# Expert products written to PSUM instead of a held row read from PSUM, with two gather buffers that come free later

## What is computed

```
h   = x + merged @ w_o ;  hn = rms_norm(h, g_ffn)
s   = scores of 8 heads against two sets of 128 sub-keys; top 16 pairs per head -> experts e, gates g
u   = u_tab[e] ;  act = gelu(sum_d hn[d] * u[e, d])          # 128 experts for each token
v   = v_tab[e] ;  y = h + sum_e g * act * v[e, :] ;  out = rms_norm(y, g_fin)
```

## Time and profile before

| | before |
|---|---|
| median of 3 runs | 1904.86 us (1900.15 to 1910.61) |
| span of the profiled execution | 2029.6 us |
| busy: TensorE / VectorE / GpSimd / ScalarE | 1467.7 / 1202.8 / 1067.7 / 380.8 us |
| DMA over the span | mean 348 GB/s, 706 MB |
| quad 0, quad 38, quad 64, quad 96, quad 124 begin at | 388, 891, 1213, 1590, 1921 us |

### The profile page before, as it was taken

How to read it: one execution, slowest core, us unless ns; L and a number is a source line. 1 busy time by engine, 2 the same in 40 slices (tenths; PEclk the granted TensorE clock), 3 DMA queues, 4 the chain that set the end, 5 groups by cost and what they waited for, 6 DMA issues and landing times.

```text
span 2029.6 us, 18882 instructions
## 1 busy us (share of the span) xinstructions
PE 1467.7 (72%) x5470; PEld 670.5 (33%) x5470; DVE 1202.8 (59%) x3335; ACT 380.8 (19%) x923; POOL 1067.7 (53%) x1082
## 2 busy tenths in 40 slices
PE   8999998756886687768996555555555666676657
PEld 5444443443443333322442222222222233221111
DVE  1034352585577567667666776677676777687541
ACT  2113441222222222111111111211111212111101
POOL 3020000264575566766566666666666666666674
PEclk9999999976897888778997877777777777776778
DMA  9999998697999799999999989999999999998997
GB/s 329 359 310 365 362 318 304 199 323 260 389 388 362 274 375 343 396 397 375 396 364 403 376 332 344 342 365 361 368 352 368 347 352 357 354 361 332 369 369 284
DMA packets 226136, 706.43 MB, mean 348 GB/s; under 512 B 21153, under 2 KB 46657, under 8 KB 226009
## 3 DMA queue, kind: packets, MB, share of 16 engines
q0 software_dynamic: 166912, 612.40, 80.5%
q1 hardware_dynamic: 59120, 92.82, 13.2%
HBM read 700.65 MB, written 72.61 MB: 381 GB/s over the span
## 4 chain that ended last, share of the span: by engine, by line
PE 26%; DVE 23%; issue 19%; DMA 11%; POOL 9%; another core or an unknown queue 8%; ACT 1%; SPq 1%; DVEq 0%; POOLq 0%; ACTq 0%
PE bank L1059 7%; PE bank L947 4%; DVE XS L1463 4%; POOL WR L660 4%; DVE GT L1463 3%; DMA arena<-in_peer_u_dram,e_all 3%; PE bank L1175 3%; POOL XS L660 2%; DMA WR<-in_peer_v_dram,arena 2%; DVE arena L1463 2%; PE bank L1076 2%; PE bank L1196 2%; PE bank L1154 2%; DMA WR<-in_w_in_dram 2%
## 5 line engine op out<-in xcount | busy, mean ns | idle before, releaser
L1059 PE MATMUL bank<-WR,arena 128*64 128x512 f32 x1728 | 536.1, 724 | 189.8 <-issue 82.1
L660 POOL DMA_INDIRECT WR<-in_peer_v_dram,arena x432 | 427.0, 988 | 301.0 <-issue 145.4
L660 POOL DMA_INDIRECT XS<-in_peer_u_dram,e_all x258 | 269.2, 1043 | 225.7 <-DVE XS L1463 77.4
L1059 PEld LDWEIGHTS bank<-WR,arena 128*64 128x64 f32 x1728 | 146.8, 163 | 520.2 <-issue 470.2
L1463 DVE SCALAR_TENSOR_TENSOR XS<-XS,bank 128x1024 f32<-128x1024 f32 x144 | 171.2, 1218 | 41.3 <-DMA XS<-in_peer_u_dram,e_all 38.8
L1463 DVE SCALAR_TENSOR_TENSOR GT<-GT,bank 128x1024 f32<-128x1024 f32 x126 | 150.0, 1218 | 59.8 <-DMA GT<-in_peer_u_dram,e_all 45.3
L1463 DVE SCALAR_TENSOR_TENSOR XS<-XS,GT 128x1024 f32<-128x1024 f32 x114 | 137.4, 1225 | 80.1 <-DMA XS<-in_peer_u_dram,e_all 65.6
L660 POOL DMA_INDIRECT GT<-in_peer_u_dram,e_all x126 | 123.1, 977 | 52.3 <-issue 33.9
L660 POOL DMA_INDIRECT arena<-in_peer_u_dram,e_all x128 | 127.4, 995 | 42.1 <-issue 37.8
L754 ACT ACTIVATE XS<-bank 128x256 f32<-128x256 f32 (+1 forms) x90 | 36.2, 405 | 469.1 <-remote 267.7
L1076 PE MATMUL bank<-WR,XS 128*128 128x512 f32 x256 | 116.0, 607 | 0.4 <-ACT arena L754 0.4
(11 more groups left out here) (234 smaller groups left out, 2122.9 us busy)
## 6 DMA issues: line engine op xcount, KB each, us to landing
out_dram<-in_cache_a_k_dram POOLq DMA_DIRECT2D x8, 4064.0 KB, 54.6
out_dram<-in_cache_a_v_dram POOLq DMA_DIRECT2D x8, 4064.0 KB, 55.4
WR<-in_w_in_dram SPq DMA_DIRECT2D x8, 2048.0 KB, 25.7
GT<-in_w_peer_q_dram SPq DMA_DIRECT2D x14, 1024.0 KB
WR<-in_w_out_dram SPq DMA_DIRECT2D x6, 2048.0 KB
WR<-in_peer_v_dram,arena POOLq DMA_INDIRECT x432
WR<-in_w_branch_a_dram SPq DMA_DIRECT2D x6, 1024.0 KB, 7.6
WR<-in_w_branch_b_dram SPq DMA_DIRECT2D x6, 1024.0 KB, 9.7
```

The costliest lines, as they stand in the source:

```text
L660: nc.gpsimd.indirect_dma_start(dst, None, table, bass.IndirectOffsetOnAxis(ap=idx, axis=0))\
L1059: last = nc.tensor.matmul(b[c][R * j:R * j + R, :], diag[p // QUAD % 4][:, s % 4, :], V[V_AT[s]][:, c * CHUNK:(c + 1) * CHUNK], start=Fals ...
```

## The change

The held copy goes, with its semaphore. Every SCALAR_TENSOR_TENSOR reads `hidden[t]` from SBUF in all quads. From quad 38 on its unread products go to the two PSUM banks (`aside`) instead of over the u row, in the sampled quads too. As all of them write the same place, each one from the second on waits until the one before has finished (`u_used` >= s). `hidden[1]` is in use until quad 63 and `hidden[2]` until quad 95, so the buffers that lie on them come later: the u ring has 7 buffers from quad 44 (with `O` as the seventh) and 8 from quad 66; the v ring has 10 from quad 56 and 12 from quad 98. `ring` hands new buffers out first and then keeps the order of use.

```diff
-HELD_FROM = {t: max(t * TILE_Q, 38) for t in range(1, TILES)}
+ASIDE_FROM = 38
@@
-WIDER_U, WIDER_V, WIDEST_V = 44 * QUAD, 56 * QUAD, 80 * QUAD
-def u_buffer(s):
-    return s % 4 if s < WIDER_U else s % 8
-def v_buffer(s):
-    if s < WIDER_V:
-        return s % 8
-    return (s - WIDER_V) % 10 if s < WIDEST_V else (s - WIDEST_V + 10) % 12
+U_AT, U_FILL, U_OLD = ring(TILES * SLOTS + DEC, {0: 4, 44 * QUAD: 7, 66 * QUAD: UR})
+V_AT, V_FILL, V_OLD = ring(TILES * SLOTS + DEC, {0: 8, 56 * QUAD: 10, 98 * QUAD: VR})
@@
-        U += [hidden[0], resid[0], hidden[1], O]
+        U += [hidden[0], resid[0], O, hidden[1]]
@@
-        held = pair[:, :]
+        aside = pair[:, :]
@@ fetch_u
+                elif U_AT[s] == 7:
+                    pool.wait_ge(S["u_used"], 2 * SLOTS)
                 elif U_AT[s] == 6:
-                    pool.wait_ge(S["held"], 1)
-                elif U_AT[s] == 7:
                     emptied(pool, "post", TILES - 1, 0)
                     emptied(pool, "post", TILES - 1, 1)
@@ fetch_v
                 elif V_AT[s] == 10 and V_OLD[s] is None:
-                    pool.wait_ge(S["held"], 2)
+                    pool.wait_ge(S["u_used"], 3 * SLOTS)
@@
-            def hold(t):
-                for i in range(2):
-                    emptied_scores = nth(TILES - 1, NH - 2 + i) + 1
-                    dve.wait_ge(free[i], emptied_scores)
-                dve.wait_ge(S["u_used"], HELD_FROM[t] * QUAD)
-                V_.tensor_copy(held, hidden[t]).then_inc(S["held"], 1)
-                dve.wait_ge(S["held"], t)
+            def product(s, u):
+                if s < ASIDE_FROM * QUAD:
+                    return u
+                if s > ASIDE_FROM * QUAD:
+                    dve.wait_ge(S["u_used"], s)
+                return aside
 
             def quad(q):
-                if q in HELD_FROM.values():
-                    hold(q // TILE_Q)
+                if q == ASIDE_FROM:
+                    for i in range(2):
+                        dve.wait_ge(free[i], nth(TILES - 1, NH - 2 + i) + 1)
@@
-                        row = held if q >= HELD_FROM[1] else hidden[q // TILE_Q]
-                        V_.scalar_tensor_tensor(u, u, 1.0, row, ALU.mult, ALU.mult,
+                        V_.scalar_tensor_tensor(product(s, u), u, 1.0, hidden[p // SLOTS], ALU.mult, ALU.mult,
                                                 accum_out=dots[:, p // TOPK % 4, p % TOPK:p % TOPK + 1]).then_inc(S["u_used"], 1)
@@
-                        V_.scalar_tensor_tensor(u, u, 1.0, hbc[b], ALU.mult, ALU.mult,
+                        V_.scalar_tensor_tensor(product(s, u), u, 1.0, hbc[b], ALU.mult, ALU.mult,
                                                 accum_out=sdots[:, 0, b:b + 1]).then_inc(S["u_used"], 1)
```

More of the change, by code:

```diff
@@ L225, with ring @@
 MIX_ORDER = {t: i for i, t in enumerate((0, 1, 2, SAMPLE, 3))}
-def ring(slots, buffers):
-    where, filled, before, last = [], [], [], {}
+def ring(slots, sizes):
+    order, where, filled, before, last = [], [], [], [], {}
     for s in range(slots):
-        b = buffers(s)
+        if s in sizes:
+            order = list(range(len(order), sizes[s])) + order
+        b = order.pop(0)
+        order.append(b)
         where.append(b)
@@ L239 @@
 UR, VR = 8, 12
-WIDER_U, WIDER_V, WIDEST_V = 44 * QUAD, 56 * QUAD, 80 * QUAD
-def u_buffer(s):
-    return s % 4 if s < WIDER_U else s % 8
-def v_buffer(s):
-    if s < WIDER_V:
-        return s % 8
-    return (s - WIDER_V) % 10 if s < WIDEST_V else (s - WIDEST_V + 10) % 12
-U_AT, U_FILL, U_OLD = ring(TILES * SLOTS + DEC, u_buffer)
-V_AT, V_FILL, V_OLD = ring(TILES * SLOTS + DEC, v_buffer)
+U_AT, U_FILL, U_OLD = ring(TILES * SLOTS + DEC, {0: 4, 44 * QUAD: 7, 66 * QUAD: UR})
+V_AT, V_FILL, V_OLD = ring(TILES * SLOTS + DEC, {0: 8, 56 * QUAD: 10, 98 * QUAD: VR})
 def hybrid_step_kernel(nc, x_p, x_s, cak, cav, cbk, cbv, g_mix, w_in, w_a, w_b, w_o, sink, g_ffn, w_pq, subk,
@@ L399, in hybrid_step_kernel @@
                   "id_in", "es_in", "es_out", "es_in_s", "es_out_s", "sg", "swm", "tT", "kd", "eps", "g_out", "ga_in", "gb_in",
-                  "eV", "vi", "wS", "sel", "copies_b", "held"):
+                  "eV", "vi", "wS", "sel", "copies_b"):
             sem(n)
```

## The result

The changed kernel took 1949.31 us (median of 4 runs, 1941.46 to 1964.20) against 1903.07 us for the kernel before: ratio 1.0268, 95% interval 1.021 to 1.0325. Repeated later it took 1956.39 us, ratio 1.0266 (1.0226 to 1.0306), which is +51 us.

The account below looks back on a forecast made before the run. VectorE in its own order was taken to set the pace behind quad 60 or so. The terms 2 + 16 - 4 + 17 + 4 gave +35 us, a median of 1940 us (+1.8%), with an 8-in-10 range of 1900 to 1985 us.

Parts of the forecast that it names:

- Theory A: Formed after the result: gathers meeting products with two SBUF inputs get longer, GpSimd's slack is used up and GpSimd binds.
- What bounds the kernel: Behind quad 60 or so VectorE in its own order sets the pace, with GpSimd and transfers close behind.
- PSUM output, 2 us: Reading both inputs from SBUF and writing products to PSUM lengthens 360 prompt instructions slightly: 2 us, bounds 0 to 4.
- Waits, 16 us: Products from quad 38 on no longer overlap: 0.13 us for each of 149, 16 us counting, bounds 0 to 38.
- Held copies, -4 us: Three copies on VectorE's path at quads 38, 64 and 96 go, each 1.26 us with its wait: 4 us gained.
- GpSimd beside two SBUF inputs: Late gathers slow from 0.961 to 1.089 us, 94 us more of GpSimd's time, of which 17 us show.
- Buffers, 4 us: Fewer u buffers in quads 44 to 65 and v buffers in 80 to 97: 4 us, from 0 to 14.
- GpSimd becomes the bound: Rival: late gathers need 1020 us, the unprofiled stretch is about 975 us: 1976 us in total; chance 0.20.
- a rate above 361 GB/s: Sign against the forecast: such a DMA rate in the late stretch would mean that the writes mattered.
- hidden: Rival: queued transfers set the pace and cover slower gathers and waits, only copies' 4 us go: 1901 to 1910 us; 0.18.
- the writes' way out of SBUF: Rival: products no longer written to SBUF free the transfers, 1883 us at a fourth of the rate difference; faster has 0.12.

Follow-up runs that it names:

- before, again: The kernel before the change, unchanged, run and profiled a second time: 1902.22 us, ratio 0.999.
- waits alone: Kernel before plus only the wait of each product for the one before it, from quad 38's second slot on: 1902.24 us, ratio 1.0005.
- rows from SBUF: Changed kernel without its waits and PSUM output: rows read from SBUF, products over the u row, buffers late: 1930.66 us, ratio 1.0135.
- before (2029.6 us): First profile of the unchanged kernel before, on which the prediction rests; that profiled execution took 2029.6 us, the median was 1904.86 us.
- second run, slow chip: Changed kernel, late products reading the PSUM bank instead of the normed row, so one SBUF input: 2033.15 us, ratio 1.0027; kernel before took 2026.76 us there.
- first run, slow chip: Changed kernel with late products over the u row and a one-column PSUM write ahead of each: 2031.66 us, ratio 1.0044; kernel before took 2026.76 us there.
- every second product: Kernel before with late buffers, no waits, and every second slot behind quad 38 reading its row from SBUF: 1918.91 us, ratio 1.0067.
- two memsets: Kernel before with two tiny GpSimd memsets ahead of every gather from quad 38 on, each waiting for the one before: 1963.17 us, ratio 1.0304.
- and an empty instruction: Changed kernel with products over the u row, waits kept, and an empty VectorE instruction behind each wait: 1932.24 us, ratio 1.0151.
- and waits: Changed kernel with products over the u row instead of PSUM; SBUF rows, waits and late buffers kept: 1933.11 us, ratio 1.0153.

## Why the forecast held, and which steps of it did not

**The account that the runs give.** GpSimd's need in the late stretch is its gathers' busy time and 0.305 us between two. From the window rows, in us:

```
                        gathers busy   + 0.305 us x count   need   stretch   rest
before, again              705            224                929     993      64
waits alone                704            224                928     991      63
rows from SBUF             770            222                992    1012      20
changed kernel             795            222               1017    1042      25
changed kernel, again      801            221               1022    1047      25
before (2029.6 us)         702            223                925    1088     163
second run, slow chip      697            222                919    1095     176
first run, slow chip       785            222               1007    1093      86
```

The rest is what the stretch leaves. As long as the need stays well below the stretch, more of it costs nothing. On the chips with 1903 us, from about 960 us of need on (every second product: 743 + 222 = 965 of 1000), the stretch is the need and 20 to 35 us; where between 929 and 965 us this begins isn't measured. With two memsets, 1.367 us x 727 and 19 us of excess give 1013 of 1041. Theory A carries the whole loss: the changed kernel's need is 88 to 93 us greater, 49 to 54 us of it show in the stretch, and the rest was slack. The kernels with waits and products over the u row and with products to PSUM differ by 989 against 1017 to 1022 us of need, 28 to 33 us, and by 21 us of time.

**Why the place of the output matters then.** The gathers in step with the products take the products' spacing less 0.305 us:

```
                            products apart   gather in step   spacing - 0.305
rows from SBUF                 1.27-1.29       0.97-0.98        0.97-0.99
and an empty instruction         1.325           1.02             1.020
and waits                        1.338           1.03             1.033
and a small PSUM write           1.370         1.06-1.07          1.065
changed kernel                   1.396         1.08-1.10          1.091
```

This holds whether the product goes to SBUF or to PSUM. PSUM output puts the waiting products 1.396 instead of 1.338 us apart, and each gather in step inherits the 0.06 us. That is shown for these gathers; they make 11 to 13 of the 28 to 34 us by which the excess grew (20.6 to 31.2 and 33.7 us in the two profiles of the changed kernel). The rest is in gathers over 1.13 us (63 us in 106 gathers, to 81 in 129 and 89 in 145), and why there are more of them is not separated. A PSUM write isn't needed for it: with output in SBUF and products 1.37 us apart, on the slow chip, they are 134 with 80 us.

Now the prediction's steps, in its order.

**What bounds the kernel: wrong.** "VectorE in its own order sets the pace" was read from the earlier trace rows of a profile 6.5% longer than the timed runs, and I carried the difference over "as it is". In the kernel at 1903 us the transfers set it behind quad 38 (share 1.02, 401 GB/s, 40% of the whole chain). The first profile resembles the slower chip: stretches of 1088 and 1095 us, shares of 0.95, 362 and 360 GB/s, and VectorE waits put down to `remote` (104 us, and 95 us in the second run there). What makes that chip slower the records don't show.

**PSUM output, 2 us: its size right, its effect missed.** 1234 ns against 1218 in the earlier trace rows is 0.016 x 360 = 6 us of VectorE, which had time. The step took the duration for the cost. The spacing grew by 0.06 us and reached GpSimd by the gathers in step, part of 21 us.

**Waits, 16 us: nothing alone** (+1 us, -4 to +6). The forecast of spacing was too small, 1.25 to 1.28 for 1.334, and the effect too large, since VectorE wasn't the bound: the lower end of the range, 0, held. The Trainium skill ("VectorE: DVE Perf Modes", on the DRAIN) has a semaphore cost nothing extra. The time agrees with that, the spacing does not: 1.27 to 1.29 us became 1.33. The same section adds that an instruction that nothing holds starts earlier, and the trace agrees with 1.14 us; so the prediction set these starts against a rule that allows them.

**Held copies, -4 us: not seen by itself.** The kernels without them are all slower for the gathers' reason.

**GpSimd beside two SBUF inputs: the amount right, the share wrong.** 94 us were forecast, from the earlier trace rows; 795.4 - 727 x 0.961 = 97 us came. The mean is 1.094 us (1.089 forecast). The Trainium skill's rule ("SBUF - State Buffer", Who interferes with whom) held at each test: 0.96 us with one input from SBUF, 1.02 with every second product at two, 1.06 to 1.10 with all. But 17 us of it were to show, by GpSimd's share of the chain; about 50 did. The share of the chain tells what a little more costs, and not what 97 us cost with 64 to 74 us of slack. On the slow chip, whose slack is that of the profile I read, 88 us more cost nothing clear of the noise (2031.66 against 2033.15 us). The reading of the earlier trace rows was wrong too: the gather of 1.99 us was held by one product, not by two. It began 0.05 us behind the start of the product at 830.54, and ended 0.81 us behind its end.

**Buffers, 4 us: nothing** (+1 us, -4 to +5).

**So the sum was right by its errors.** +35 against +46 and +51 us: 16 + 4 - 4 + 2 us that don't show as such, and some 33 too few for the gathers. The mechanism was the rival's, "GpSimd becomes the bound", and its own first term, 1020 us of need against a shorter stretch, +45 us, is 1950 us: what was measured. But that agreement is in part luck: the stretch was 993 us and not 975, so need less stretch is 27 us, and GpSimd was still idle for 25 us of it. The 26 us that it added for waits and buffers didn't come. It had 0.20; the two lines of the page that already disagreed, 2029.6 us and 1904.86, should have given it the most. Of the prediction's signs, the one for it came (GpSimd almost without waits), and two misled, as both were numbers of the slow profile: the span was to be near 2065 us and was 1945.5, and a rate above 361 GB/s was to mean that the writes mattered; 378 came. The other rivals: transfers did pace the kernel before, as "hidden" had it, but couldn't cover a slower GpSimd; and the writes' way out of SBUF freed nothing, 401 GB/s fell to 378.

## What to carry to other kernels

Before a sum is made on a profile, set its span beside the timed runs: with 6.5% between them, another resource may set the pace, and slack read there is not the slack of the runs. For an engine off the path, compare what is added to its need (busy time and the gap that it can't avoid) with the length of the stretch; the loss begins where the two meet, not in proportion to its share of the chain. A VectorE instruction with two SBUF inputs is paid for by GpSimd's gathers; one input in PSUM, by a copy of 1.2 us per tile, kept 26 us here, and 51 us together with what PSUM output adds once both inputs are in SBUF.

## What the runs showed of the hardware

A gather held back ends a fixed time after the product that held it: 0.806 to 0.814 us after the end of a product that writes SBUF (10th to 90th percentile of gathers over 1.0 us, five kernels with rows from SBUF), 0.799 to 0.807 us for one that writes PSUM. In the changed kernel each of the 352 gathers over 1.0 us ends so, 324 behind a product and 28 behind another instruction with two SBUF inputs. One product is enough for the largest, 1.93 to 1.99 us: they began 0.04 to 0.10 us behind its start. The same follows other instructions with two SBUF inputs: `eq<-iota,bposf` of the lists and the diagonals `arena<-idG,wS` are behind 35 of the 44 gathers over 1.0 us in the late stretch of the copy of the kernel before.

The gathers fall into step with the products by themselves, 201 to 218 of 749 in the changed kernel: each is released by a product's end, and 0.305 us after its own end the next runs into the next product. For these, a change to the spacing on VectorE, by output or wait, changes GpSimd's pace by as much.

One GpSimd memset of 0.12 us between two gathers is free (cycle 1.249 for 1.246 us); two of 0.28 us together cost 0.12.
